# Hybrid decoder step on one core: one row of gather steps for all passes, and the first pass's tile 0 ahead of tile 1 from attention's output to its first scores

## The reference, cut to what matters

```python
def _peer(h, w_pq, sub_keys, peer_u, peer_v):
    q = einsum('td,de->te', t, w_pq).reshape(T, 8, 2, 128)
    s = einsum('thpk,hpnk->thpn', q, sub_keys)
    s1, i1 = top_k(s[:, :, 0], 16)
    s2, i2 = top_k(s[:, :, 1], 16)
    cand = s1[..., :, None] + s2[..., None, :]
    top_s, pos = top_k(cand.reshape(T, 8, 256), 16)
    idx = take_along_axis(cidx, pos)              # 8 heads x 16 = 128 experts a token
    g = softmax(top_s)
    a = gelu(einsum('td,ted->te', t, peer_u[idx]))
    out = einsum('te,ted->td', g * a, peer_v[idx])
```

## The kernel before, in words

| pass, job | before | after |
|---|---|---|
| 0, heads 1, 3, 5, 7 scored | 0, 8, 18, 29 | 0, 14, 24, 36 |
| 1, first projection "v", mixer's output "mo", first query | 53, 142, 210 | 58, 139, 202 |
| 1, heads 5, 6, 7 scored; heads end | 248, 254, 255; 261 | 240, 246, 247; 253 |
| 2, "v", first query | 332, 538 | 325, 522 |
| 3, "v", first query | 610, 802 | 600, 778 |
| first steps of passes 1, 2, 3, end | 264, 592, 856, 1184 | 256, 576, 832, 1160 |

## Time and profile before

### The profile page before, as it was taken

The page is one execution under the profiler, slowest core; times in us unless marked ns, Lnnn a source line. Parts: engine busy times, 40 slices in busy tenths (PEclk is TensorE's granted clock), DMA queues, the critical chain, the costliest instruction groups (busy, mean ns, idle before and its releaser), DMA issues.

```text
span 4493.5 us, 36583 instructions
## 1 busy us (share of the span) xinstructions
PE 3483.6 (78%) x11076; PEld 2069.9 (46%) x11076; DVE 3193.4 (71%) x6067; ACT 887.3 (20%) x2681; POOL 2737.7 (61%) x2318
## 2 busy tenths in 40 slices
PE   9999989998789678775658989887679575555555
PEld 6876636674546235663345546554436221111111
DVE  2111578977867888887786899877877877666665
ACT  1001231121212221112122311211213222111111
POOL 0000275666657687787676666776657578777775
PEclk9999999899889898887878989798889888676766
DMA  5343599999999899999999989999999799999998
GB/s 193 114 159 140 229 345 337 355 394 346 364 373 398 302 334 366 398 397 408 402 399 361 372 322 384 343 405 366 369 394 366 272 333 329 370 376 373 370 351 308
DMA packets 461419, 1518.69 MB, mean 338 GB/s; under 512 B 41124, under 2 KB 45540, under 8 KB 461224
## 3 DMA queue, kind: packets, MB, share of 16 engines
q0 software_dynamic: 331776, 1208.11, 71.1%
q1 hardware_dynamic: 129448, 308.25, 18.3%
HBM read 1508.97 MB, written 7.23 MB: 337 GB/s over the span
## 4 chain that ended last, share of the span: by engine, by line
PE 31%; POOL 26%; DVE 16%; issue 13%; DMA 12%; ACT 1%; another core or an unknown queue 1%; DVEq 0%; SPq 0%; POOLq 0%; ACTq 0%
PE ps L851 15%; POOL vrow L767 13%; POOL urow L767 13%; DMA vrow<-in_peer_v_dram,idx 10%; PE ps L870 8%; PE ps L826 5%; DVE X L1342 4%; DVE urow L1331 3%; DMA urow<-in_peer_u_dram,idx 2%; PE ps L840 1%; PE ps L988 1%; PE ps L1015 0%; DVE RB L1654 0%; PE ps L966 0%
## 5 line engine op out<-in xcount | busy, mean ns | idle before, releaser
L767 POOL DMA_INDIRECT urow<-in_peer_u_dram,idx x1152 | 1385.0, 1202 | 1212.1 <-DVE idx L1549 504.5
L1331 DVE CUSTOM_DVE_ANT_0 urow<-urow,T 128x1024 f32<-128x1024 f32 x1152 | 1405.1, 1223 | 535.2 <-DMA urow<-in_peer_u_dram,idx 471.1
L767 POOL DMA_INDIRECT vrow<-in_peer_v_dram,idx x1152 | 1350.7, 1172 | 523.1 <-issue 318.0
L826 PE MATMUL ps<-vrow,diag 128*128 128x512 f32 x1792 | 1043.2, 721 | 508.0 <-DMA vrow<-in_peer_v_dram,idx 445.9
L851 PE MATMUL ps<-RH,W 128*128 128x256 f32 (+1 forms) x4608 | 1184.1, 418 | 173.8 <-DVE RH L1587 50.7
L851 PEld LDWEIGHTS ps<-RH,W 128*128 128x128 f32 x4608 | 903.1, 197 | 458.9 <-issue 56.4
L1342 DVE SCALAR_TENSOR_TENSOR X<-vrow,wts,X 128x1024 f32<-128x1024 f32 x704 | 905.9, 1287 | 159.8 <-issue 134.6
L826 PEld LDWEIGHTS ps<-vrow,diag 128*128 128x128 f32 x1792 | 369.7, 221 | 1131.2 <-issue 1060.8
L1119 ACT ACTIVATE gel<-dots 128x4 f32<-128x4 f32 x288 | 59.0, 205 | 2157.3 <-DVE dots L1331 1800.0
L870 PE MATMUL ps<-W,RB 128*128 128x512 f32 (+1 forms) x576 | 258.6, 610 | 25.1 <-issue 11.2
L851 PE MATMUL ps<-RB,W 128*128 128x256 f32 (+1 forms) x1024 | 251.5, 406 | 2.8 <-DVE RV L1688 2.3
(11 more groups left out here) (245 smaller groups left out, 2325.5 us busy)
## 6 DMA issues: line engine op xcount, KB each, us to landing
W<-in_w_in_dram SPq DMA_DIRECT2D x56, 2048.0 KB
W<-in_w_pq_dram SPq DMA_DIRECT2D x16, 2048.0 KB
urow<-in_peer_u_dram,idx POOLq DMA_INDIRECT x1152
vrow<-in_peer_v_dram,idx POOLq DMA_INDIRECT x1152
W<-in_w_a_out_dram SPq DMA_DIRECT2D x8, 2048.0 KB
W<-in_w_b_out_dram SPq DMA_DIRECT2D x8, 2048.0 KB
W<-in_w_mix_o_dram SPq DMA_DIRECT2D x8, 2048.0 KB
W<-in_w_xq_dram SPq DMA_DIRECT2D x8, 2048.0 KB
```

Source lines behind the costliest of these rows:

```text
L767: return pool.indirect_dma_start(ring[:, slot, :], None, table, bass.IndirectOffsetOnAxis(ap=idx[:, q % TSLOT, e:e + 1], axis=0))
L826: o = pe.matmul(ps[:, bank + b, :], diag[:, pe_turn[m] % NDIAG, :], vrow[:, m % NV, b * 512:(b + 1) * 512], start=m in pe_first, stop=m in ...
L1331: dve.tensor_tensor_reduce(urow[:, m % NU, :], urow[:, m % NU, :], T[:, q % TSLOT, :], 1.0, 0.0, ALU.mult, ALU.add, dots[:, n % WRING, m % ...
```

## The change

Two parts.

1. **One row of steps.** `step_base(p)` becomes `pick_base(p)`: step m has the dot of pick m and the sum of pick m - 8, whatever the pass. There are 1160 steps. GpSimd's gathers, the dots, the places, the merges of TensorE's spans (now 9 steps after a pass's last pick) and the start of passes 2 and 3's trunks (LAG + 2) follow. A span of the next pass can begin while the last one isn't merged, and then waits for it on TensorE.
2. **Pass 0, tile 0 first.** Attention's output, projection, norm, and the queries and scores of heads 0 and 1 are done for tile 0 alone ("o", "xo" 0, "n" 2 0, "pq" 0 to 3, "sc" 0 and 1), and then for tile 1 ("oo", "xo" 1, "fh", "n" 2 1, "pr" 0 to 3, "sd" 0 and 1); heads 2 to 7 are done for both tiles as before. FIRST goes from 40 to 46 and the places of the scores move.

```diff
-FIRST = 40
+FIRST = 46
 def step_base(p):
-    return sum(pass_picks(q) + LAG for q in range(p))
+    return pick_base(p)
+STEPS_IN_ALL = sum(pass_picks(p) for p in range(2 * DEPTH)) + LAG
...
     jobs += [(("o", c), "act", 1, 1) for c in range(KC)]
+    if p == 0:
+        jobs += [(("xo", 0), "dve", 2, 1)] + [(("oo", c), "act", 1, 1) for c in range(KC)]
+        jobs += [(("sk", 0), "dve", 2, 1), (("sk", 1), "dve", 2, 1), (("fg",), "dve", 2, 1), (("n", 2, 0), "dve", 2, 1)]
+        for h in range(2):
+            jobs += [(("pq", c), "act", 1, 1) for c in (2 * h, 2 * h + 1)] + [(("sc", h), "act", 2, 1)]
+        jobs += [(("xo", 1), "dve", 2, 1), (("fh",), "dve", 2, 1), (("n", 2, 1), "dve", 2, 1)]
+        jobs += [(("pr", c), "act", 1, 1) for c in range(BLK)] + [(("sd", h), "act", 2, 1) for h in range(2)]
+        for h in range(2, PH):
+            jobs += [(("pq", c), "act", 1, fm) for c in queries_before(h, 2)] + [(("sc", h), "act", 2, 2)]
+        return jobs
...
-        score = {("sc", h): (0, 0, 3, 8, 13, 18, 24, 29)[h] for h in range(PH)}
+        score = {("sc", h): (0, 0, 8, 14, 19, 24, 30, 36)[h] for h in range(PH)}
...
-    begin, end = step_base(p - 1) + (FIRST if p == 1 else OVER), step_base(p)
+    begin, end = step_base(p - 1) + (FIRST if p == 1 else LAG + 2), step_base(p)
...
-            span(b + n - CLOSE, b + n, step_base(p + 1) + 2, lambda m: p % 2 or m % 4)
+            span(b + n - CLOSE, b + n, step_base(p + 1) + LAG + 1, lambda m: p % 2 or m % 4)
...
-            for p in range(2 * DEPTH):
-                for step in range(pass_picks(p) + LAG):
-                    m = pick_base(p) + step
-                    if step < pass_picks(p):
...
+            for m in range(STEPS_IN_ALL):
+                if m < len(picks):
+                    if m == 0 or turn_of_pick(m) > turn_of_pick(m - 1):
+                        pool.wait_ge(idx_done, turn_of_pick(m))
+                    if m >= NU:
+                        pool.wait_ge(u_read, m - NU + 1)
+                    gather(tables[0], urow, m % NU, m).then_inc(u_in[m % NU], 16)
+                if m >= LAG:
+                    v = m - LAG
+                    if v >= NV:
+                        await_sum(pool, v - NV)
+                    gather(tables[1], vrow, v % NV, v).then_inc(v_in[v % NV], 16)
...
+                    prompt_output("o", 0, P)
+                    await_evac(pe, (0, "o", KC - 1))
+                    add_tile(0)
+                    prompt_output("oo", P, 2 * P)
+                    subkey_transposes()
+                    pe.wait_ge(ffn_in, 16)
+                    spread((0, "fg"), FFN_ROW, KC, 0)
+                    norm_transposes(2, 0)
+                    for h in range(2):
+                        for c in (2 * h, 2 * h + 1):
+                            tile_queries("pq", c, 0)
+                        await_evac(pe, (0, "pq", 2 * h + 1))
+                        scores((0, "sc", h), h, [0])
+                    await_evac(pe, (0, "oo", KC - 1))
+                    add_tile(1)
+                    spread((0, "fh"), FFN_ROW, KC, 0)
+                    norm_transposes(2, 1)
+                    for c in range(BLK):
+                        tile_queries("pr", c, 1)
+                    await_evac(pe, (0, "pr", BLK - 1))
+                    for h in range(2):
+                        scores((0, "sd", h), h, [1])
...
+                    add_to_x("xo", 0)
+                    turn_subkeys()
+                    dve.wait_ge(sq_first, 1)
+                    tile_norm(0, (0, "fg"))
+                    top_group(0, 0)
+                    top_group(0, 1)
+                    add_to_x("xo", 1)
+                    dve.wait_ge(sq_done, 3)
+                    tile_norm(1, (0, "fh"))
+                    for k in range(2, len(head_groups(0))):
+                        top_group(0, k)
```

218 lines of the change are left out of this document (144 added, 74 removed).

## The result

Measured beside 20 runs of the kernel before (median 4526.1 us), the changed kernel takes 4542.33 us (4516.93 to 4560.24, 20 runs). The ratio is 1.0041, 95% interval [1.0028, 1.0055]: slower by 0.4%, some 18 us by the ratio and 16 us by the medians, where 19 us faster was forecast. The two profiled executions are not equally good samples. That of before (4495.19 us) is faster than all its 20 timed runs, that of after (4557.72 us) is the second longest of its 20, so the 62 us between their traces overstate the difference more than three times.

The account below looks back on a forecast made before the run. It took DMA gathers as the main bound (2.9 us a step), with TensorE bounding pass 1's trunk and VectorE the boundaries. Terms 7.5 - 14.5 - 43 + 31 = -19 us gave a median of 4505 us, range 4455 to 4548.

Parts of the forecast that it names:

- Part 1, the first gather: Start of pass 0: tile 0's sum at 461.1, first selection at 478.9, first gather at 488.3, 19 us earlier.
- Part 1, what it costs: Rest of pass 0: heads 2 and 3 selected at about 547, pass 1's trunk starting 7.5 us later (-5 to +12).
- Part 2: Pass 1's trunk, mixer's output to first query: five fewer steps beside it save 14.5 us; ends 0 and -37.7.
- Part 3: Trunks of passes 2 and 3: eight fewer steps each, on DMA, save 43 us together; ends -46 and -20.
- Part 4: The three pass boundaries: 8 more dots each on a busy VectorE add 31 us in all; ends 0 and +70.
- The slower case: Pass 0's delay reaches TensorE-bound trunk 1 if TensorE's clock is lower; boundaries at upper end: +47, 4571 us; chance 0.12.
- DMA was the limit all along: From the first gather on, DMA share is about 0.96, so reordering gathers only moves idle time: 4520 us; chance 0.13.
- The boundaries close: At the boundaries gathers and selections share the holes at no cost, and trunk 1 shrinks by all its steps: 4451 us; chance 0.27.
- the first gather isn't earlier: In pass 0, projection weights or banks come late and add delay: 4510 us, counted inside the forecast, no chance of its own.

Follow-up runs that it names:

- e10: The changed kernel run once more, unaltered, on a faster chip: 4435.12 us, ratio 1.0036 to the kernel before.
- e16: The kernel before with only the scores' places moved earlier (0, 0, 3, 7, 11, 15, 20, 25), FIRST left at 40: 4419.81 us, ratio 1.0010.
- e5: The kernel before with FIRST = 46 in place of 40 and nothing else: 4427.32 us, ratio 1.0027.
- e11: The changed kernel with FIRST back at 40 and the scores' places moved, tile 0 still first: 4432.47 us, ratio 1.0025 to the kernel before.
- e9: The kernel before with one row of steps alone, FIRST = 40, on a faster chip: 4429.22 us, ratio 1.0027.
- e12: The kernel before with FIRST = 34 and earlier scores, so pass 1's trunk begins six steps earlier: 4408.60 us, ratio 0.9971.
- e4: The changed kernel with all of the last 56 sums of passes 0 and 2 on TensorE: 4556.11 us, ratio 1.0060 to the kernel before.
- e7: The kernel before with one row of steps, and head 1's scores ahead of queries 4 and 5: 4432.71 us, ratio 1.0038.
- e8: The kernel before with one row of steps, and tile 1 of pass 2 selected 21 steps later: 4427.29 us, ratio 1.0026.
- e14: The kernel before with one row of steps, FIRST = 34 and earlier scores: 4403.59 us, ratio 0.9976.
- e1: The kernel before with one row of steps alone, FIRST = 40, on the slower chip: 4526.83 us, ratio 0.9984.
- e15: The kernel before with pass 0's tile 0 first, old rows of steps, FIRST = 34 and scores moved: 4420.06 us, ratio 1.0012.

## Why the prediction was wrong

**Part 1, the first gather: nearly right.** 461.1 forecast for tile 0's sum, 460.79 measured; 478.9 and 482.10 for the first selection; 488.3 and 491.47 for the gather. The output matmuls of half width took 6.68 us (6.5 taken), half of the projection 14.00 (13.9). From the sum to the selection it took 21.3 us for 17.8. Of these 3.5 us TensorE's clock is 2.9: the first two narrow queries ran at a granted clock of 0.51, in 6.64 us for the 3.6 that I had taken (rows in the last section).

**Part 1, what it costs: the first term that failed.** I had +7.5 us for the start of pass 1's trunk, bounds -5 to +12. It is +22.2 (679.18 - 656.94), and +21 in e10 against e16 (676.78 - 655.78). Two steps of the working are short. (a) Heads 2 and 3 at 547; they come at 552.75, because ScalarE's copy of the scores stands behind diagonals that wait for TensorE's first sums, a wait I hadn't priced. (b) "3 us less" than 97.1 us from there to the last index; it is 103.6 us (552.75 to 656.39), 9.5 more than taken. The rings weren't full at that time but starved: the DMA share from 491 to 553 is 0.86, since GpSimd stood 11.12 and 15.21 us. Of the delay of the last index, e5 shows 15 us for FIRST = 46 alone (644.82 - 629.69 in e16; 11 against before, on a slower chip) and e11 against e9 10 us for tile 0 first (639.71 - 629.35).

**Part 2, -14.5 us: wrong.** From the mixer's output to the first query pass 1's trunk took 294.4 us after and 286.8 before, by the GpSimd rows of steps 139 to 202 and 142 to 210. In e10 against e16 it is 279.4 for 284.1. So five steps fewer gave between 5 us and nothing, where 14.5 were counted. I had named that end ("0, if TensorE's 232 of 282 us with its waits are the bound there too") and chosen against it. The first part was 356.0 for 358.7 us, as forecast.

**Part 3, -43 us: the other term that failed, a quarter of it came.** From the boundary to its first query pass 2's trunk took 15.2 us less: 23.1 less from "v" to the first query, as forecast for the whole, and 7.9 more ahead of "v". Pass 3's trunk took 5.5 us more, where I had 20 less and had named 0 as an end. The hole of the second boundary moved to that trunk's start: the 16 steps from the boundary to "v" took 67.9 us, where the 10 of before took 37.7. Between picks 700 and 760 e9 took 234.9 us and e12 221.7 on the same chip, with TensorE busy 74% in both and DMA at 0.96 for 1.00; what holds that stretch isn't shown. On the faster chips the five old-row traces and the seven with one row give 882.7 and 864.3 us for pass 2 (-18) and 748.1 and 747.1 for pass 3 (-1), so -19 in all for the -43.

**Part 4, +31 us: about right.** From the last index of pass 1's heads to pick 264 it is 23.8 us, against 14.0 before, and 24.0 in e9 against 13.7 in e12: +10 us, with 10.5 forecast. The second and third boundary were 14.4 and 11.2 us longer by the GpSimd rows, from a pass's first query to the 8th step of its retrieval, 62 steps in either kernel, so about 36 us for 31. On the faster chips it is 11.7, 15.1 and 9.2 us, again 36. Gathers did fill the holes, and the boundaries got longer all the same. The size came as forecast; that it is VectorE's 8 more dots isn't shown, and e4 speaks against it, since easing VectorE alone doesn't shorten them.

**The sum.** With the terms as measured: 22.2 - 2.7 + 7.6 - 15.2 + 5.5 + 36 = +53 us, of the 62 between the two profiled executions; the other 9 lie behind the last boundary, where both kernels do the same 320 steps, and are probably spread between executions. By many runs the whole is some 16 to 18 us. Parts 3 and 4 together were forecast at -12 us and are +17 on the faster chips (column B above). What is wrong by sign in the traces of before and after, and not only by size, is part 2 and pass 3's trunk; on the faster chips they are -5 and -1 us. In both I had let steps count that had other work beside them: TensorE's in pass 1, and in pass 3 a hole at the start.

**The range.** The median lies inside 4455 to 4548, and that is luck: its upper end stood for a part 4 of +70 us, which measured 36, and the time came from parts 1 to 3 instead. The sum behind that end is also off by 4 us (4505 + 39 = 4544).

**The rivals.** The slower case named the right mechanism, TensorE carrying pass 0's delay over, with 20 us and part 2 at 0, both near what was measured. Its condition was another one, TensorE at its lower clock: that cost 2 us at tile 1's queries (the first 20 records of 128 columns 0.21 us apart and the rest 0.11), and the granted clock from 553 to 656 us was 0.97. It was too high in the boundaries (+70 for 36), so it ended at 4571 and was given 0.12. *DMA was the limit all along* would let no trunk's start matter, and e5 and e12 move the time by 0.3% each way; its case also passed over the three holes, at 182 to 231 GB/s. *The boundaries close* fell with part 4, and *the first gather isn't earlier* with part 1.

**What stays open.** What one row of steps costs in all hangs on the start of pass 1's trunk: on the faster chips 1.0027, 1.0038 and 1.0026 at 40 (e9, e7, e8), and 0.0005 above e12 at 34 (e14); why it differs wasn't found. On the slower chip e1 stood at 0.9984 with an interval of 0.004 and the traces overlap, so there it isn't settled. Tile 0 first is worth 0.000 by the ratios of e11 and e9 and costs 0.004 in e15 against e12 (two chips); it gains nothing in any form tried. By the ratios the losses of `FIRST = 46` (0.27%) and of one row (0.27%) don't add up to more than 0.36% in e10; the traces have 36 us between e16 and e10, but e10's profiled execution is its longest. VectorE's wait of 11.12 us in pass 0 was not taken away by any run.

## What to carry to other kernels

A transfer that starts earlier is worth only what reaches the next bound: ask which stage behind it has no slack, what starts that stage, and whether the edit moves that instant. Here one such stage was pass 1's trunk, which TensorE fills for 365 of 367 us, and a single number (e5 and e12) moved the time about two thirds as much as the whole change did. When a stage is bounded by an engine, count the fewer steps beside it as nothing until a trace shows otherwise, and try the number that sets its start in both directions before rewriting what lies ahead of it. And a hole that is filled isn't yet time gained: one row filled three holes, lengthened the three boundaries by 36 us and shortened the trunks between them by 19.

## What the runs showed of the hardware

**Chips differ in how fast they gather.** The kernel before takes 4526 and 4529 us beside the changed kernel and e1 to e4, and 4414 to 4417 us on the three chips of e5 to e16, 2.5% less. Where gathers alone run, the row of e12 reads

```profile
3900.00:4400.00 500.00, 285.62 (x391) 89.23 (x389) 354.26 (x477) 85.18 (x340) 375.38 (x375) 0.74 1.01 399
...
2000.00:2100.00 100.00, 56.82 (x248) 48.05 (x246) 74.16 (x100) 26.08 (x52) 63.45 (x55) 0.83 1.03 407
```

399 GB/s where before has 364, but 407 against 405 in a stretch of pass 2's trunk. Most of the difference lies where nothing but gathers of random rows runs: of the 86 us between the traces of before and e16, 62 are behind step 864. From pick 900 to 1151 it is 676.8 us in e12 against 729.2. What makes a chip slower there isn't shown.

**A gather's issue isn't always 0.94 us.** That is the median of the 2304 issues of after, and their mean is 1.21. Where VectorE was busy 27.22 of 30 us, single issues on GpSimd took 5.93, 2.88, 3.16 and 4.87 us (2658 to 2679 in after), about 13 us more than four usual ones. Whether VectorE's load does it was not tried.

**What looks like a price of narrow queries is the clock.** Tile 0's queries for head 0 and for head 1 are each 32 records of 128 columns. Their rows in after, and below them two stretches inside them, columns as above:

```profile
473.93 6.64 PE L1065 MATMUL ps<-RH,W 128*128 128x128 f32 x32 [1.32 <-DVE RH L1883]
481.49 3.74 PE L1065 MATMUL ps<-RH,W 128*128 128x128 f32 x32
...
473.90:480.00 6.10, 6.07 (x29) 6.08 (x30) 0.00 (x0) 0.28 (x1) 0.00 (x0) 0.51 0.00 0
481.50:485.10 3.60, 3.60 (x34) 3.53 (x32) 2.84 (x16) 0.66 (x2) 0.00 (x0) 1.00 0.00 0
```

In the first TensorE had come out of waits of 1.45 and 1.32 us, the granted clock is 0.51 (the lower of its two levels, 1.2 GHz), and the records start 0.213 us apart. In the second it is 1.00 and they start 0.111 us apart, half of the 0.216 us of the 256 columns of before. Those ran at 1.00 too. So here the time went with the columns at one clock, and for head 0 nearly all that half the columns could save (7.17 to 6.64 us) was lost to the lower clock.
